# The 32 sample tokens go ahead of the 256 prompt tokens from the second norm on

## The reference, cut to what matters

```python
xp = xp + merge_groups(ya, yb, yc, yd, out_g[l], w_out[l])
xp = xp + cross_attend(rmsnorm(xp, norm_g[l, 1]), ca_wq[l], ca_wo[l], mk, mv)
xp = xp + peer_ffn(rmsnorm(xp, norm_g[l, 2]), peer_wq[l], peer_keys[l], peer_u[l], peer_v[l])
...
def peer_ffn(xn, wq, keys, u_tab, v_tab):
...
        q = (xt @ wq).reshape(PEER_BLOCK, PEER_HEADS, 2, PEER_DK // 2)
        s = jnp.einsum('phcd,hcnd->phcn', q, keys).astype(jnp.float32)
        top_s, top_i = lax.top_k(s, PEER_TOPK)
...
        best_s, best_j = lax.top_k(cand_s, PEER_TOPK)
        e_idx = jnp.take_along_axis(cand_i, best_j, axis=-1)
        gate = jax.nn.softmax(best_s, axis=-1)
        act = jax.nn.gelu(jnp.einsum('pd,phkd->phk', xt, u_tab[e_idx]).astype(jnp.float32),
                          approximate=False)
        return jnp.einsum('phk,phkd->pd', gate * act, v_tab[e_idx].astype(jnp.float32))
```

## Time and profile before

| | us |
|---|---|
| median of 3 runs | 1321.83 (1321.82 to 1322.94) |
| the profiled execution | 1319.55 |
| its span, first to last instruction | 1317.7 |
| PE busy | 824.7 (63%) |
| DVE busy | 665.7 (51%) |
| POOL busy | 378.8 (29%) |
| ACT busy | 352.2 (27%) |
| bytes moved by DMA | 392.60 MB, of which 306.24 MB on POOL's queue |

### The profile page before, as it was taken

How to read it: one execution, slowest core, us unless ns; L and a number is a source line. 1 busy time by engine, 2 the same in 40 slices (tenths; PEclk the granted TensorE clock), 3 DMA queues, 4 the chain that set the end, 5 groups by cost and what they waited for, 6 DMA issues and landing times.

```text
span 1317.7 us, 16379 instructions
## 1 busy us (share of the span) xinstructions
PE 824.7 (63%) x5964; PEld 463.2 (35%) x5964; DVE 665.7 (51%) x1693; ACT 352.2 (27%) x984; POOL 378.8 (29%) x382
## 2 busy tenths in 40 slices
PE   6998899886889998974443344433444334444443
PEld 5777777563667676751000010000100001000010
DVE  2363224453220311437666666665666666676553
ACT  3232211342121202123322232222322223232322
POOL 0410030720000000226443344433444344444440
PEclk9999997898899999986555555555555555555555
DMA  8431123822637944559999999999999999999995
GB/s 304 129 97 33 59 97 96 314 77 70 210 106 293 354 133 133 205 203 423 426 426 400 399 424 427 425 405 385 421 426 426 402 399 425 426 426 426 426 425 236
DMA packets 99519, 392.60 MB, mean 298 GB/s; under 512 B 9168, under 2 KB 55440, under 8 KB 60016
## 3 DMA queue, kind: packets, MB, share of 16 engines
q0 software_dynamic: 43520, 306.24, 56.4%
q1 hardware_dynamic: 53616, 83.22, 18.6%
q10 hardware_dynamic: 2304, 2.10, 0.5%
HBM read 381.38 MB, written 5.42 MB: 294 GB/s over the span
## 4 chain that ended last, share of the span: by engine, by line
DMA 50%; PE 35%; DVE 7%; ACT 5%; issue 2%; POOL 1%; ACTq 0%; SPq 0%; DVEq 0%; POOLq 0%
DMA RB<-peer_uv,idx 41%; PE ps L661 13%; PE ps L675 7%; DMA RA<-peer_uv,idx 6%; PE ps L1184 2%; DMA W<-peer_wq 2%; DVE RB L2059 1%; PE ps L775 1%; DVE RA L2059 1%; PE ps L665 1%; ACT dg L1513 1%; PE ps L1099 1%; PE ps L1113 1%; PE ps L1134 1%; PE ps L965 1%
## 5 line engine op out<-in xcount | busy, mean ns | idle before, releaser
L1184 PE MATMUL ps<-RA,dg 128*32 128x256 f32 x1424 | 188.4, 620 | 247.2 <-ACT dg L1513 246.3
L2144 POOL DMA_INDIRECT RA<-peer_uv,idx x178 | 189.1, 1062 | 359.7 <-PE ps L1184 227.0
L1184 PE MATMUL ps<-RB,dg 128*32 128x256 f32 x880 | 118.0, 628 | 166.8 <-ACT dg L1513 166.8
L2059 DVE CUSTOM_DVE_ANT_0 RA<-RA,gr 128x1024 f32<-128x1024 f32 x119 | 145.7, 1224 | 88.9 <-DMA RA<-peer_uv,idx 88.6
L1507 ACT ACTIVATE gl<-act 128x1 f32<-128x1 f32 x288 | 58.3, 203 | 480.1 <-DVE act L2059 479.8
L1184 PEld LDWEIGHTS ps<-RA,dg 128*32 128x32 f32 x1424 | 41.0, 138 | 391.9 <-issue 391.3
L661 PE MATMUL ps<-xT,W 128*128 128x288 f32 x672 | 171.3, 415 | 8.3 <-DMA W<-peer_wq 6.4
L2144 POOL DMA_INDIRECT RB<-peer_uv,idx x110 | 120.4, 1095 | 189.1 <-PE ps L1184 155.1
L661 PEld LDWEIGHTS ps<-xT,W 128*128 128x128 f32 x672 | 128.8, 194 | 45.0 <-DMA W<-peer_wq 6.9
L2059 DVE CUSTOM_DVE_ANT_0 RB<-RB,gr 128x1024 f32<-128x1024 f32 x73 | 89.4, 1224 | 65.0 <-DMA RB<-peer_uv,idx 65.0
L1184 PEld LDWEIGHTS ps<-RB,dg 128*32 128x32 f32 x880 | 25.8, 139 | 257.7 <-issue 257.7
(11 more groups left out here) (390 smaller groups left out, 1131.0 us busy)
## 6 DMA issues: line engine op xcount, KB each, us to landing
W<-w_in SPq DMA_DIRECT2D x11, 1024.0 KB, 5.3
MR<-mk_s SPq DMA_DIRECT2D x8, 1024.0 KB, 13.9
MR<-mv_s SPq DMA_DIRECT2D x8, 1024.0 KB, 12.5
W<-peer_wq SPq DMA_DIRECT2D x8, 1024.0 KB, 5.6
W<-ca_wk SPq DMA_DIRECT2D x4, 1024.0 KB, 5.5
W<-ca_wv SPq DMA_DIRECT2D x4, 1024.0 KB, 5.7
W<-w_out SPq DMA_DIRECT2D x4, 1024.0 KB, 6.7
W<-ca_wq SPq DMA_DIRECT2D x4, 1024.0 KB, 5.0
```

Source lines behind the costliest of these rows:

```text
L1184: ins = mm(acc(c, q), dg[:, p % 4, :], slot(p, 1)[:, 256 * q:256 * q + 256], start=False, stop=False, skip_group_check=True)
L2059: V.tensor_tensor_reduce(out=slot(p, 0), in0=slot(p, 0), in1=xrep(c), scale=1.0, scalar=0.0, op0=ALU.mult, op1=ALU.add, accum_out=act_k[:, ...
L2144: G.indirect_dma_start(both(p), None, io["peer_uv"], bass.IndirectOffsetOnAxis(ap=idx3[:, n % 3, k:k + 1], axis=0))\
```

## The change

From `w_out` on, sample and prompt are separate. The sample unit of each `w_out` block comes first; the sample's norm, its `ca_wq`, its attention, its `ca_wo`, its `peer_wq`, scores and searches go ahead, with the prompt's attention in between; then come the prompt's `ca_wo`, norm and `peer_wq`. So `ca_wq`, `ca_wo` and `peer_wq` are loaded twice, 16 MB more, as forms "S" and "TS" (sample) and "F" and "TP" (prompt).

```diff
@@ -45,10 +45,14 @@
     + [("ca_wk", 256 * i, 256, "F") for i in range(4)]
     + [("ca_wv", 256 * i, 256, "T") for i in range(4)]
     + [("w_out", 256 * i, 256, "T") for i in range(4)]
+    + [("ca_wq", 256 * i, 256, "S") for i in range(4)]
     + [("ca_wq", 256 * i, 256, "F") for i in range(4)]
-    + [("ca_wo", 256 * i, 256, "T") for i in range(4)]
+    + [("ca_wo", 256 * i, 256, "TS") for i in range(4)]
+    + [("peer_wq", 256 * h, 256, "S") for h in (0, 2, 4, 6, 1, 3, 5, 7)]
+    + [("ca_wo", 256 * i, 256, "TP") for i in range(4)]
     + [("peer_wq", 256 * h, 256, "F") for h in (0, 2, 4, 6, 1, 3, 5, 7)]
 )
+WOUT, WQS, WQP, WOS, PQS, WOP, PQP = 20, 24, 28, 32, 36, 44, 48
 RING = 3
 GAP = 3
 NIT = 18
...
-        + [("lin", b) for b in range(20, 24)] + [("norm", 0)] + [("lin", b) for b in range(24, 28)]
-        + [("scross_k", None), ("cross", None), ("scross_v", None)] + [("lin", b) for b in range(28, 32)] + [("norm", 1)]
-        + [("lin", b) for b in range(32, 36)] + [("score", 0)] + [("lin", b) for b in range(36, 39)]
-        + [("gate", 0), ("lin", 39), ("score", 1), ("peer", None)])
+        + [("lin", WOUT), ("lin", WOUT + 1), ("lin", WOUT + 2), ("unit", (WOUT + 3, 0)), ("unit", (WOUT + 3, 1)),
+           ("part", 0), ("unit", (WOUT + 3, 2)), ("norm_s", 0)]
+        + [("small", b) for b in range(WQS, WQS + 4)] + [("turned", WQS + 3), ("norm_p", 0), ("lin", WQP), ("scross_k", None)]
+        + [("lin", b) for b in range(WQP + 1, WQP + 4)] + [("scross_v", None), ("cross", (0, 2))]
+        + [("lin", b) for b in range(WOS, WOS + 4)]
+        + [("cross", (2, 4)), ("part", 1), ("cross", (4, 6)), ("norm_s", 1), ("cross", (6, 7)), ("small", PQS),
+           ("cross", (7, 8)), ("small", PQS + 1), ("cross", (8, 9)), ("small", PQS + 2), ("cross", (9, 10)),
+           ("small", PQS + 3), ("cross", (10, 11))]
+        + [("small", b) for b in range(PQS + 4, PQS + 8)] + [("turned", PQS + 7), ("score_s", None)]
+        + [("topk", (0, 0, 9)), ("unit", (WOP, 0)), ("topk", (0, 9, 14)), ("gate", 0), ("unit", (WOP, 1)),
+           ("topk", (1, 0, 5)), ("unit", (WOP + 1, 0)), ("grow", 0), ("topk", (1, 5, 10)), ("unit", (WOP + 1, 1)),
+           ("topk", (1, 10, 14)), ("lin", WOP + 2), ("unit", (WOP + 3, 0)), ("pick", 1), ("unit", (WOP + 3, 1)), ("pick", 1),
+           ("norm_p", 1), ("pick", 2)]
+        + [x for b in range(PQP, PQP + 4) for i in range(2) for x in (("unit", (b, i)), ("pick", 1))]
+        + [("score", 0)]
+        + [x for b in range(4) for i in range(2) for x in
```

In form "S" the 32 sample tokens are the stationary side and the weights move, in four quarters (two halves of the columns, even and odd chunks); ScalarE copies the result to `st`, and a product with `halfsum` turns it and adds even and odd (`turned`, one block later). On TensorE:

```diff
-                ins = mm(PS[:, u % 2, 0:a.shape[2]], w[:, cc:cc + nn], a[:, k, :], start=k == 0, stop=k == KC - 1)
+                n = T if b >= WQP else a.shape[2]
+                ins = mm(PS[:, u % 2, 0:n], w[:, cc:cc + nn], a[:, k, 0:n], start=k == 0, stop=k == KC - 1)
+            elif t == "s":
+
+                for half in range(2):
+                    q = 2 * half + k % 2
+                    ins = mm(PS[TS * q:TS * q + TS, u % 2, 0:P], a[:, k, T:N], w[:, half * P:(half + 1) * P],
+                             start=k < 2, stop=k >= KC - 2, skip_group_check=True)
...
+        def turned(b):
+
+            u = unit_of(b, 0)
+            i = small_index(u)
+            pe.wait_ge(*at("act_lin", ("unit", u + 1)))
+            mm(PS[:, u % 2, P:P + 2 * TS], st[:, i % 2, :], cst("halfsum"), start=True, stop=True,
+               skip_group_check=True).then_inc(S.sem("pe_turn"), 1)
+
+        def small(b):
+
+            ready(b)
+            for k in range(KC):
+                product(unit_of(b, 0), k)
+            if b not in (WQS, PQS):
+                turned(b - 1)
```

SP's list: `mk_s` goes ahead of the sample's weights, `mv_s` ahead of the prompt's last block of `ca_wq`, and the copies of `XN` are gone:

```diff
+        for r in range(2):
             sp.dma_start(gr[:, r, :], io["gains"][r:r + 1, :].to_broadcast([P, D])).then_inc(S.sem("gr_in"), 16)
+        load_block(23)
+        for b in (0, 2, 4, 6, 1, 3, 5, 7):
+            sp.dma_start(MR[:, b, :], io["mk_s"][b]).then_inc(S.sem(f"mr{b}_in"), 16)
+        for b in range(24, 31):
+            load_block(b)
         sp.dma_start(MK[:], io["o_memk"].rearrange("(c p) m -> p c m", p=P)).then_inc(S.sem("mk_in"), 16)
         sp.dma_start(MV[:], io["o_memv"].rearrange("(k p) n -> p k n", p=P)).then_inc(S.sem("mv_in"), 16)
-        for b in range(23, 28):
+        for b in (0, 2, 4, 6, 1, 3, 5, 7):
+            sp.wait_ge(*at("pe_mr", ("k", b)))
+            sp.dma_start(MR[:, b, :], io["mv_s"][b]).then_inc(S.sem(f"mr{b}_in"), 16)
+        for b in range(31, 35):
             load_block(b)
-        for name in ("mk_s", "mv_s"):
-            for b in (0, 2, 4, 6, 1, 3, 5, 7):
-                if name == "mv_s":
-                    sp.wait_ge(*at("pe_mr", ("k", b)))
-                sp.dma_start(MR[:, b, :], io[name][b]).then_inc(S.sem(f"mr{b}_in"), 16)
-        for b in range(28, 31):
+        sp.dma_start(keys[:], io["keysT"]).then_inc(S.sem("keys_in"), 16)
+        for b in range(35, 44):
             load_block(b)
-        sp.wait_ge(*at("dve_cx", "ys"))
-        sp.dma_start(keys[:], io["keysT"]).then_inc(S.sem("keys_in"), 16)
+        sp.wait_ge(*at("pe_cx", ("sc", len(CUNITS) - 1)))
         for q in range(4):
             sp.dma_start(gfin[32 * q:32 * q + 32, :], io["gains"][2:3, 256 * q:256 * q + 256].to_broadcast([32, 256]))\
                 .then_inc(S.sem("gf_in"), 16)
-        for b in range(31, 36):
+        for b in range(44, 56):
             load_block(b)
```

The samples are iterations 0 and 1. Their 32 gathers use the eight slots of `RA` (now over `MR`); gathers 32 to 36 go into `RB` and wait for the last scores (`pe_s` 9 of 9), and POOL issues in order:

```diff
     def iteration(n):
 
-        if n >= 16:
-            return 8, n - 16
-        return n // 4 * 2 + n % 2, n % 4 // 2
+        if n < 2:
+            return 8, n
+        return (n - 2) // 4 * 2 + n % 2, (n - 2) % 4 // 2
...
+
+    def slot_number(p):
+
+        return p % EARLY if p < 32 else (p - 37) % NSLOT
 
     def slot(p, half):
...
         for p in range(NIT * TOPK):
             n, k = divmod(p, TOPK)
             if k == 0:
                 pool.wait_ge(S.sem("topk_done"), n + 1)
-            if EARLY <= p < NSLOT:
-                pool.wait_ge(S.sem("pe_s"), 10)
-            elif p >= NSLOT:
+            if EARLY <= p < 32:
+                pool.wait_ge(S.sem("pe_free"), p - EARLY + 1)
+            elif 32 <= p < 37:
+                pool.wait_ge(S.sem("pe_s"), 9)
+            elif p >= 37:
                 pool.wait_ge(S.sem("pe_free"), p - NSLOT + 1)
```

`xrep` is filled by TensorE (a product with a piece of the identity) and ScalarE (a copy from PSUM). The picks are a stage of their own: 20 of them stand in `ORDER` between units of the prompt's `ca_wo` and `peer_wq`, the other 268 in `peer`. On TensorE, then ScalarE:

```diff
+        def replicate(c):
+
+            if 1 < c < 8:
+                pe.wait_ge(S.sem("act_xr"), place(c))
+            a = 32 * (c % 4)
+            for half in range(2):
+                for j in range(4):
+                    ins = mm(PS[32 * j:32 * j + 32, xr_bank(c) + half, :], ident[a:a + 32, a:a + 32],
+                             XN[a:a + 32, c // 4, half * 512:(half + 1) * 512], start=True, stop=True,
+                             skip_group_check=True)
+            ins.then_inc(S.sem("pe_xr"), 1)
 
...
+        def pick(count):
+
+            for p in range(picked[0], picked[0] + count):
+                n, k = divmod(p, TOPK)
+                c, _ = iteration(n)
+                pe.wait_ge(*landed(p))
+                pe.wait_ge(S.sem("act_dg"), p + 1)
+                for q in range(4):
+                    ins = mm(acc(c, q), dg[:, p % 4, :], slot(p, 1)[:, 256 * q:256 * q + 256], start=False,
+                             stop=False, skip_group_check=True)
+                ins.then_inc(S.sem("pe_free"), 1)
...
+            picked[0] += count
+
         def peer():
 
-            pe.wait_ge(S.sem("act_s"), 10)
-            for c in range(9):
+            pe.wait_ge(S.sem("act_s"), 9)
```

```diff
+        def pick(count):
+            for p in range(picked[0], picked[0] + count):
+                n, k = divmod(p, TOPK)
+                act.wait_ge(S.sem("dve_dot"), p + 1)
+                if p >= 4:
+                    act.wait_ge(S.sem("act_dg"), p - 3)
+                A(gl[:, p % 4:p % 4 + 1], act_k[:, n % 2, k:k + 1], ACT.Gelu).then_inc(S.sem("act_gl"), 1)
+                if k == 0:
+                    act.wait_ge(S.sem("dve_gg"), n + 1)
+                if p >= 4:
+                    act.wait_ge(S.sem("pe_free"), p - 3)
+                act.wait_ge(S.sem("act_gl"), p + 1)
+                A(dg[:, p % 4, :], gat[:, n % 2, k, :], ACT.Copy, scale=gl[:, p % 4:p % 4 + 1])\
+                    .then_inc(S.sem("act_dg"), 1)
+                if (n, k) in XR_AT:
```

More of the change, by code:

```diff
@@ L68, in linear_units @@
             units += [(b, 128 * j, 128, None) for j in range(2)]
+        elif form == "S":
+            units.append((b, 0, n, "s"))
+        elif name in ("w_out", "ca_wo"):
+            units += [(b, 0, n, t) for t in {"T": (2, 0, 1), "TS": (2,), "TP": (0, 1)}[form]]
         else:
@@ L287, in sbuf_map @@
     put("MV", 2, D)
-    put("MR", B, KC * MEM)
     put("SCx", 3, 256)
@@ L1438, in cross @@
+        def cross(first, end):
             nu = len(CUNITS)
-            for s in range(nu + 2):
+            for s in range(first, min(end, nu + 2)):
                 if s < nu:
@@ new lines, in _ @@
+        picked = [0]
+        def pick(count):
[12 more added lines that the diff above has]
```

(59 more changed lines are left out.)

630 lines of the change are left out of this document (337 added, 293 removed).

## The result

The changed kernel takes 1357.38 us (median of four runs, 1351.41 to 1361.64), the kernel before 1321.82 in the same comparison: a ratio of 1.0269, 95% interval 1.0242 to 1.0295. The direction was predicted; the time was not: 1334 was forecast and the range ended at 1356. The profiled execution took 1361.64, its span is 1359.7, where the sum gave 1330.3.

What follows compares the result with a forecast made beforehand. The end was taken as set by when all tokens' scores are done plus the gathers left: 1317.7 + 81.6 (later start) + 1.0 - 70.0 (gather-part savings) = 1330.3 us span, 1334 as a median; range 1303 to 1356.

Steps and rivals of the forecast that it cites:

- The term for the copies: Gather part: moving the copies of XN from DMA to TensorE and ScalarE saves 20.8 us.
- The pick cycle: Prompt's peer_wq: each of sixteen units of 3.55 us, followed by a sample pick, takes 5.25 us, 84.0 us in all.
- starving weights: Rival, chance 0.08: beside gathers, eight peer_wq blocks take 21.9 us each instead of 10.5; 91 us more, 1425.
- the falling clock between units: Rival, chance 0.10: stops between peer_wq units lower PE's clock, 3.55 + 0.45 us more a unit; 64 us, 1398.
- the hidden picks: Rival, chance 0.20: ScalarE and PE overlap, so waits in peer_wq units and ca_wo picks vanish; 27 us less, median 1307.
- the prediction's sum of the first part: Marks from w_out through the sample's scores and top-k, added up to put the first gather at 513 us.
- the pace: Gather part: one gather of 1.049 MB at 426 GB/s takes 2.461 us.
- the allowance for the clock: TensorE standing still in five other places costs 0 to 9 us at the lower clock; 4 us taken, scores done at 661.
- the weights behind the 8 MB transfers: ca_wq weights queue on SP behind mk_s and mv_s: fourth small block issued at 392, last prompt block stalls 5.6 us.
- the stretch from the sample's ca_wo to its scores: Attention steps, sample peer_wq blocks, sum of parts, transposes and some 10 us of waits: from 464.8 to 502.
- the fourth block of the prompt's ca_wo: Its weights, issued at 512.5 just ahead of eight gathers, were booked with 18.5 us, between bounds 4.9 and 21.9.
- 20 gathers fewer behind the scores: Sample picks between projection units leave 260 gathers behind the last score instead of 280, saving 49.2 us.

Runs made afterwards that it cites:

- the standard: The changed kernel run once more, unchanged, and profiled a second time: 1356.64 us, ratio 1.0262.
- Extra products: The changed kernel with unread products in TensorE's first-part waits, cut to the idle time left there: 1339.22 us, ratio 1.0124.
- the new order: The changed kernel with SP's transfers reordered: half of mk_s behind five ca_wq blocks, the prompt's last ca_wq block ahead of mv_s: 1343.42 us, ratio 1.0158.
- both edits: The changed kernel with SP's transfers reordered and the fewer unread products, none before the last ca_wq block: 1329.42 us, ratio 1.0060.

## Why the prediction was wrong

*Right: what bounds the kernel and which way it goes.* The end is set by when all scores are done plus the gathers left. The term for the copies (20.8) is 19.1 by itself. The pick cycle (5.25) is 5.36. The clock does not fall between units: stops of 1.07 us leave the cycle at 5.36 (behind stops of 2.49 to 3.95 us three units of the first profile ran slowly; behind the same 2.49 us in the second profile the unit did not). Two dear rivals, starving weights and the falling clock between units, did not come about, nor did the hidden picks. On the clock rival the Trainium skill (TensorE: Matmul & The Clock Gate, HAM oscillation — how this bites in real kernels) describes short runs of products between DMA waits that each start slow. The traces agree in the first part (stops of up to 8.38 us, and 0.58 granted from 385 to 410, where TensorE is busy for 16.35 of 25 us). The stops between peer_wq's units, 1.07 us and for ScalarE's diagonal, are not such waits, and the cycle held at 5.36.

The step that failed is the prediction's sum of the first part, up to the first gather: 513 was forecast, and the standard has 536.89, 23.9 us more. Three of its terms were too small, the first two by the experiments, the third by the marks; the pace behind them is a fourth.

*Wrong, first: the allowance for the clock.* The step "0 to 9 in all, I take 4" counted five places. The chain after has more of them, since each wait for weights is one as well: X1 (6.41 for a unit that takes 3.67 elsewhere), the small blocks (1.94 for 1.01), the prompt's first block (9.39 for 7.1), the last (8.77 for 7.1), the last small blocks, the scores and the copy behind them. Extra products took 11.5 us off the first gather, and 14.7 where the new order was in place too (524.51 to 509.84). So 11.5 to 14.7 us of the delay at the first gather are this step; the allowance of 4 stood behind that mark, so 7 to 11 are left at the late one.

*Wrong, second: the weights behind the 8 MB transfers.* I saw the queue (a stall of 5.6 us at the last ca_wq block, the fourth small block at 392) but took each wait by itself. The stall was 8.38, since the keys' products, which let mv_s go, ended at 425.1 instead of 416; the small blocks ended at 400.0 instead of 393. The new order gave back 12.4 us at the first gather, 4.5 more than the stall and its lower clock as booked (7.9).

*Wrong, third: the stretch from the sample's ca_wo to its scores.* It was forecast from 464.8 to 502, 37.2 us. In the chain after it goes from 477.11 (475.18 + 1.93) to 522.08, 45.0 us. With the new order and the fewer products it is still 42.6, from 456.26:

```profile
455.19 1.07 PE ps L729 x16
...
498.83 1.08 PE ps L1279 x32
```

So 5.4 us remain where the first two are mended, most of it work of TensorE that was booked too short. In the first profile it is busy for 35.6 of the 45.0 us, at a mean granted clock of 0.80, where 27.2 were booked (14.4 + 10 + 1.9 + 0.9); with both edits for 35.4 of the 42.6, at 0.92, of which 4.0 are extra products. The idle time, 9.4 us in the first profile, is near the 10 booked. The three make up the 23.9: 14.7 for the clock, 4.5 for the queue, and 4.7 that are left, about what this stretch is too long.

*Too dear: the fourth block of the prompt's ca_wo.* No stall came before it, booked with 18.5 us for its weights. They were issued at 537.6 beside the eight gathers, and the seventh of seven units on end began at 551.2, so they were in within 13.6 us. From the residuals' end to the norm it took 33.1 us in the first profile (528.43 to 561.54), forecast 43.2. The norm, copies and peer_wq behind it took longer than forecast; without slow units that leaves the 6.5 us by which the stretch between the two gathers was booked too long.

*Wrong, fourth: the pace.* 2.461 us a gather was read from slots that the change moves. At 421 GB/s it is 1.049 MB / 421 = 2.49, 260 x 0.03 = 7.8 us; the span from late gather to end is 5.0 longer than the sum, and what gave the other 2.8 back is not shown. No rival had this, and no row of the trace before shows it.

*The picks barely pay.* They were booked at 1.7 us each against 2.461 for a gather later. From the first unit to the end of the second scores it is 98.0 us in the standard (580.73 to 678.7) and 64.6 without picks: 33.4 for 16 picks, 2.1 each, since the units beside the table loads and the one behind the longest wait cost more than the cycle. What they save is 2.49. 16 x 0.4 is 6 us, as the two profiled spans have it (6.2), where the medians give 9.6 and the ratios some 13. The median of the run without picks is 5.2 above its profiled execution (1366.19 and 1361.0), that of the standard 1.8, which makes the 3.4 between spans and medians.

*What the change gives and takes.* Its gain that holds, the copies, needs no new order of tokens. The rest, 20 gathers fewer behind the scores, is paid for by a gather part that begins 106 us later in the first profile and 98.9 in the second. With queue and clock mended it is still at 1.0060 of the kernel before.

It stays open why the slots' place matters: the moved tiles were not separated one by one.

## What to carry to other kernels

A DMA piece in a chain of waits is how long the transfer was on its way, not how long the engine stood still; take idle time from the engine's own timeline before you fill or book it. Splitting one stage into small ones puts a wait between each two, and a wait is paid twice, once itself and once in the lower clock behind it, so a chain of moved marks needs an allowance for each wait and not for each stage. And when a change bundles several edits, price them alone: here one edit carried the gain, and it goes with the old order.

## What the runs showed of the hardware that I had not expected

The 280 gathers of the kernel before, with the copies by TensorE, run at 426 GB/s with the slots at one place in SBUF and at 421 with RA 41.6 KB higher in each partition (and small tiles moved to make room), in flat windows of 100 us; the 260 of the changed kernel, with RA over MR, run at 421 in every variant. 256 bytes for all tiles make no difference. And one program does not meet the same clock each time: two executions of the changed kernel agree within 0.6 us at the first gather and differ by 7.1 at the late one, 147 us further on; 5.7 us of it are three units and two copies that one of them ran slowly.
